# Two attention mixers: head units taken one at a time, or in pairs of partition halves

## The reference, cut to what matters

```
def attend(q, k, v):                      # even mixer: 8 heads on 2 key heads, all 512 keys
    s = einsum('bqhgd,bkhd->bhgqk', q, k) # context queries: 256 context keys alone
    return einsum('bhgqk,bkhd->bqhgd', softmax(s), v)

def block(b, qblk):                       # window mixer: 16 heads on 4 key heads
    s_win = where(valid, q @ k_window, -1e30)     # 128 before, 128 own, 128 after
    s_ctx = q @ k_context                         # 256 keys
    p = softmax(concat([s_win, s_ctx, sink_column]))[..., :-1]
    return p_win @ v_window + p_ctx @ v_context
```

## Time and profile before

| what | us |
|---|---|
| median of 3 runs | 2731.23 (2728.13 to 2741.21) |
| profiled execution, its own time | 2731.92 |
| its span | 2730.1 |
| PE busy | 2486.5 (91%), mean granted clock 0.956 |
| DVE busy | 1493.4 (55%) |
| ACT busy | 902.1 (33%) |
| first to last attention product, even mixer | about 949 to 1124 |
| the same, window mixer | about 2353 to 2482 |

### The profile page before, as it was taken

One profiled execution on the slowest core, in us unless ns is written; L12 is line 12 of the kernel. 1 busy time (PEld: TensorE's weight loads), 2 busy tenths in 40 slices (PEclk: granted clock), 3 DMA queues, 4 the chain that ended last, 5 costly groups with the idle time before them and its releaser, 6 DMA issues.

```text
span 2730.1 us, 41787 instructions
## 1 busy us (share of the span) xinstructions
PE 2486.5 (91%) x17450; PEld 2000.5 (73%) x17450; DVE 1493.4 (55%) x2494; ACT 902.1 (33%) x1583; POOL 76.5 (3%) x148
## 2 busy tenths in 40 slices
PE   8999999799998888777987899998999997988998
PEld 6687778588876656577875688876788875656998
DVE  5666474555544666666544655555555443573553
ACT  2331231422322444542223422223322223353542
POOL 0000000000000000000000000000000000000000
PEclk9999999999999999898989999999999998997999
DMA  7236436244444100000012244433444441101553
GB/s 286 93 136 210 169 126 221 102 139 139 140 146 156 60 33 32 0 3 4 4 43 99 104 143 139 139 139 123 139 139 139 142 151 63 62 32 61 179 181 137
DMA packets 55915, 310.78 MB, mean 114 GB/s; under 512 B 5936, under 2 KB 9392, under 8 KB 28080
## 3 DMA queue, kind: packets, MB, share of 16 engines
q1 hardware_dynamic: 32944, 224.74, 23.2%
q0 software_dynamic: 20736, 75.51, 8.4%
q10 hardware_dynamic: 2048, 7.85, 0.8%
HBM read 307.03 MB, written 1.05 MB: 113 GB/s over the span
## 4 chain that ended last, share of the span: by engine, by line
PEld 40%; PE 33%; issue 11%; DVE 9%; ACT 6%; DMA 1%; PEldq 0%; ACTq 0%; DVEq 0%
PEld bank L1293 13%; PEld bank L1286 13%; PEld bank L1289 12%; PE bank L1166 5%; PE bank L1354 3%; PE bank L1163 2%; PE bank L1225 2%; PE bank L1241 2%; PE bank L1030 2%; PE bank L1139 2%; PE bank L1037 2%; PE bank L1033 2%; ACT hn L1712 2%; PE bank L1120 1%; PE bank L1130 1%
## 5 line engine op out<-in xcount | busy, mean ns | idle before, releaser
L2153 DVE TENSOR_TENSOR w_lo<-ring,w_hi 128x1024 fp32r<-128x1024 f32 (+1 forms) x198 | 236.2, 1193 | 447.8 <-ACT w_hi L1677 447.8
L1286 PE MATMUL bank<-ffn_x_hi,w_hi 128*128 128x512 f32 x1008 | 398.7, 396 | 0.0
L1289 PE MATMUL bank<-ffn_x_lo,w_hi 128*128 128x512 f32 x1008 | 398.7, 396 | 0.0
L1293 PE MATMUL bank<-ffn_x_hi,w_lo 128*128 128x512 f32 x1008 | 398.7, 396 | 0.0
L1677 ACT ACTIVATE w_hi<-ring 128x1024 fp32r<-128x1024 f32 (+1 forms) x198 | 203.9, 1030 | 288.5 <-PE bank L1289 277.2
L2085 DVE SCALAR_TENSOR_TENSOR ms<-mod_rows,c_silu 128x1024 f32<-128x1024 f32 x200 | 244.0, 1220 | 1.2
L1293 PEld LDWEIGHTS bank<-ffn_x_hi,w_lo 128*128 128x128 f32 x1008 | 189.5, 188 | 45.7
L1286 PEld LDWEIGHTS bank<-ffn_x_hi,w_hi 128*128 128x128 f32 x1008 | 189.5, 188 | 45.7
L1289 PEld LDWEIGHTS bank<-ffn_x_lo,w_hi 128*128 128x128 f32 x1008 | 189.5, 188 | 45.6
L1286 PE MATMUL bank<-ffn_h_hi,w_hi 128*128 128x512 f32 x528 | 211.3, 400 | 0.0
L1289 PE MATMUL bank<-ffn_h_lo,w_hi 128*128 128x512 f32 x528 | 208.8, 396 | 0.0
(11 more groups left out here) (440 smaller groups left out, 4621.5 us busy)
## 6 DMA issues: line engine op xcount, KB each, us to landing
ring<-in_stream SPq DMA_DIRECT2D x211, 1024.0 KB, 4.8
mod_rows<-in_mod_stream POOLq DMA_DIRECT2D x144, 512.0 KB, 3.8
one_const<-in_one ACTq DMA_DIRECT2D x1, 1665.0 KB, 13.8
mix_const<-in_two ACTq DMA_DIRECT2D x1, 1440.0 KB, 6.2
win_const<-in_win ACTq DMA_DIRECT2D x1, 1089.0 KB, 4.8
x<-in_x SPq DMA_DIRECT2D x4, 256.0 KB, 4.4
c_silu<-in_c SPq DMA_DIRECT2D x1, 1024.0 KB, 9.9
x<-in_x SPq DMA_DIRECT2D x1, 1024.0 KB, 25.7
```

Source lines behind the costliest of these rows:

```text
L1286: mm = pe.matmul(bank[:, 0:tok], w_high, hi, start=k == 0, stop=False)
L1289: mm = pe.matmul(bank[:, 0:tok], w_high, lo, start=False, stop=False)
L1293: mm = pe.matmul(bank[:, 0:tok], w_low, hi, start=False, stop=last)
L2153: V.tensor_tensor(low[:, 0:h.nk, :], raw_half(h), high[:, 0:h.nk, :].bitcast(F32), ALU.subtract).then_inc(sem("w_split"), 1)
```

## The change

Units are reordered so that two that follow each other differ in nothing but the partition half, and `attention` is replaced in both mixers by `attention_pairs`, which takes two of them in one step. The first block keeps `attention`.

- **PE**: scores are cut in column pieces (2 of 256 in the even mixer, 2 of 192 in the window mixer) and issued alternately for the two units, each in its own bank. Value products alternate likewise, into one bank, partitions 0 to 63 and 64 to 127. Order in a step: scores of pair i, values of pair i-lag-1, transposes of pair i-lag (6 or 8 in two banks). Lag is 1 in the even mixer and 2 in the window mixer.
- **Sink and padding** become 2 score columns, a product of 4 rows (`sink_q`, `sink_k`), 2 columns wide: the mask, the maximum and the exponential's sum take them along. The steps on L2310, L2320, L1762 and L1763 go.
- **DVE**: the maximum comes out negated, so the multiplication by -1 (L2311) goes; one reciprocal serves a pair. With lag 1 a step rescales pair i-1 and then takes the maxima of pair i; with lag 2 the other way round.
- **ACT**: one copy takes a pair's product out (128 partitions). `nop`s and waits behind copies and exponentials go.
- **Places**: one pair in each of the places 6 to 17 of the even mixer, finishing steps in 18 and 19; two pairs in each of the places 5 to 10 of the window mixer, 7 steps in the tail.
- The constants of the window mixer grow from 2178 to 2432 columns of 128 partitions.

```diff
+PAIR_LAG = (1, 2)
-        units = [6 + u // 2 for u in range(24)] + [18, 19, 20]
+        pairs = [6 + n for n in range(12)] + [18, 19]
...
-        units = [5 + u // 4 for u in range(24)] + [len(main)] * 11
+        pairs = [5 + n // 2 for n in range(12)] + [len(main)] * 7
...
-            sc = [(ph4["q"][rows, j, cols], ph4["q"][rows, 8 + j // 4, P:TOK], TOK - P, [])]
+            sc = [(ph4["q"][rows, j, cols], ph4["q"][rows, 8 + j // 4, k0:k0 + 192], 192, []) for k0 in (P, P + 192)]
+            sc.append((c4("sink_q")[0:4, cols], param("sink_k", 2 * head, 2)[0:4, :], 2, []))
...
+            def attention_pairs(us, lag):          # PE
+                def step(i):
+                    if i < n:
+                        two = us[2 * i:2 * i + 2]
+                        taken = [take_bank() for _ in two]
+                        at = 0
+                        for k, (_, _, width, _) in enumerate(two[0].scores):
+                            for u, (bank, full) in zip(two, taken):
+                                lhs, rhs, _, _ = u.scores[k]
+                                mm = pe.matmul(bank[:, at:at + width], lhs, rhs, start=True, stop=True)
...
+                    if i >= lag + 1:
+                        j = i - lag - 1
+                        bank, full = take_bank()
+                        for b, use in copied[j]:
+                            pe.wait_ge(bank_free[b], use + 1)
+                        for k in range(len(two[0].outs)):
+                            for a in range(last + 1):
+                                for e, u in enumerate(two):
+                                    mm = pe.matmul(bank[p0:p0 + dv, k * P:(k + 1) * P], v, u.bufs["pT"][:, e, kt * P:(kt + 1) * P],
...
+                    if lag <= i < n + lag:
+                        j = i - lag
+                        pe.wait_ge(sem("pair_ready"), b_p + j + 1)
+                        for e in range(2):
+                            bank, full = take_bank()
+                            for kt in range(u.keys // P):
+                                mm = pe.transpose(bank[:, kt * P:(kt + 1) * P], ...
...
+                def step(i):                        # DVE
+                    if lag == 1 and 1 <= i < n + 1:
+                        rescaled(i - 1)
+                    if i < n:
+                        largest(i)
+                    if lag == 2 and 1 <= i < n + 1:
+                        rescaled(i - 1)
...
+                        V.tensor_reduce(stats[:, (2 * i + e) % 4, 0:u.parts], src, AX_X, ALU.max, negate=True).then_inc(sem("pair_max"), 1)
...
-                        if u.sink is not None:      # ACT
-                            nc.scalar.activation(stats[:, i % 4, 3:4], u.sink, ACT.Exp, bias=stats[:, i % 4, 0:1])
-                            last = nc.scalar.activation(stats[:, i % 4, 6:7], u.pad, ACT.Exp, bias=stats[:, i % 4, 0:1])
```

More of the change, by code:

```diff
@@ L122, in const_tables @@
     padding = np.where(q[:, 1, 0] >= 128, q[:, 1, 0] - 127, 0)
[L123 removed]
+    out["sink_q"] = np.zeros((P, SEQ))
+    out["sink_q"][0], out["sink_q"][1] = 1.0, np.concatenate([np.full(P, MASKED), np.log(padding)])
     out["window"] = np.concatenate([win, np.zeros_like(win)], 2).reshape(P, -1)
@@ L309, in blend_order @@
                     yield what, i
-        for i, place in enumerate(units):
+        for i, place in enumerate(pairs):
             if place == at:
-                yield "unit", i
+                yield "pair", i
         if layer == 0 and at == 19:
@@ L1013, in blend @@
                 steps = blend_steps(layer)
-                norms, scores = head_norms(steps), attention(units)
+                norms, scores = head_norms(steps), attention_pairs(units, PAIR_LAG[layer])
                 b_r = tally("heads_roped", sum(st.rope is not None for st in steps))
@@ L1072, in blend @@
                         norms(what, i)
-                    elif what == "unit":
-                        if i < len(units):
-                            pe.wait_ge(sem("heads_roped"), b_r + blend_needs(layer, i))
-                        if i == 3:
+                    elif what == "pair":
+                        if 2 * i < len(units):
+                            pe.wait_ge(sem("heads_roped"), b_r + blend_needs(layer, 2 * i))
+                        if i == PAIR_LAG[layer] + 1:
                             b, use = held["v"]
@@ L2249, in blend @@
                             turns.next()
-                    elif what == "unit":
-                        scores(i, before != "unit")
+                    elif what == "pair":
+                        scores(i)
                     elif what != "none":
                         norms(what, i)
-                    before = what
             def gated_add(bank, free, layer, v, c, tok):
@@ L2343, in attention, with attention_pairs, largest, rescaled @@
                 return step, came_out
+            def attention_pairs(us, lag):
+                n = len(us) // 2
+                read, slots = {}, 2 * lag + 2
+                def largest(i):
+                    read[i] = []
+                    for e in range(2):
+                        u = us[2 * i + e]
+                        bank, _ = full_bank()
+                        read[i].append(((turns.n - 1) % BANKS, (turns.n - 1) // BANKS))
+                        src = bank[:, 0:u.width].rearrange("p (k w) -> p k w", k=u.parts)
+                        if u.mask is not None:
+                            part = src[:, :, u.mask_at:u.mask_at + u.mask.shape[2]]
+                            link(V.tensor_tensor(part, part, u.mask, ALU.add))
+                        V.tensor_reduce(stats[:, (2 * i + e) % 4, 0:u.parts], src, AX_X, ALU.max, negate=True).then_inc(sem("pair_max"), 1)
+                def rescaled(i):
+                    u, at = us[2 * i], 2 * i % 4
+                    for b, use in read[i]:
+                        dve.wait_ge(bank_free[b], use + 1)
+                    link(V.reciprocal(stats[:, at:at + 2, 4:4 + u.parts], stats[:, at:at + 2, 2:2 + u.parts]))
+                    w = u.keys // u.parts
+                    for e in range(2):
+                        for k in range(u.parts):
+                            pk = u.bufs["p"][:, (2 * i + e) % slots, k * w:(k + 1) * w]
+                            last = V.tensor_scalar(pk, pk, stats[:, at + e, 4 + k:5 + k], None, ALU.mult)
+                    last.then_inc(sem("pair_ready"), 1)
+                def step(i):
+                    if lag == 1 and 1 <= i < n + 1:
[4 more added lines that the diff above has]
+                        rescaled(i - 1)
+                    if i >= lag + 1:
+                        turns.next()
+                    if lag <= i < n + lag:
+                        for e in range(2):
+                            turns.next()
+                return step
             def mixer(layer):
```

113 lines of the change are left out of this document (76 added, 37 removed).

## The result

The changed kernel takes 2666.56 us (median of 4 runs, 2663.92 to 2669.14) against 2732.07 for the kernel before (2728.13 to 2741.21): ratio 0.976, 95% interval 0.974 to 0.978. The gain is 65.5 us; the forecast was 40, and the time lies outside the range. The profiled execution's span is 2666.8 (before 2730.1).

What follows compares the result with a forecast made beforehand. PE, busy 91% of the span, was taken as the bound, with DVE's chain setting mixer places. Window mixer -20.7, -9.1 and -10.8, even mixer 0, constants +0.5 summed to -40: 2692 us, range 2680 to 2700.

Steps and rivals of the forecast that it cites:

- the same 0.23 each as anywhere in the feed-forward stages: Dense halves of the window mixer: 5.57 us over 24 products, read as full rate, against a clock staying at 1.2 GHz.
- place 5: Window mixer: the lag of two leaves fewer products before the dense half; 9.7 us saved, less 0.6 carried over: -9.1.
- places 6 to 10: Window mixer: DVE's path (6.29 us) ends after PE's (6.03); 4.1 saved in each of five places, -20.7.
- tail: End of the window mixer: from 32.8 us to 22, between 18.6 at full clock and 26.8; -10.8.
- Value products: Attention pairs on PE: the two column halves run side by side, 0.80 us a pair instead of 1.46.
- Even mixer: DVE's chain sets its places: -1.5 us from the pairs, +1.5 for the clock after longer waits, 0 together.
- Load of constants: Head of the window mixer: 12% more columns hold DVE up by 0 to 0.9 us; +0.5 taken.
- Serial values: Rival, window mixer: value products of a pair run one behind another; +10 us, 2702; chance 0.17.
- no overlap: Rival, window mixer: neither scores nor values of a pair overlap on PE; +20 us, 2712; chance 0.05.
- the clock that stays down: Rival: PE stays at 1.2 GHz through the window mixer; +66 us, 2758; chance 0.03.
- The clock takes back: Rival: tail slow as before in share (+4.8 us), clock falls in the even mixer (+3.9); 2701; chance 0.13.

Runs made afterwards that it cites:

- before_64: The kernel before with 16 unused columns (64 bytes) ending the parameter tile, so later tensors lie as in the changed kernel: 2701.65 us, ratio 0.988.
- ffn_64: The kernel before with 64 unused bytes ahead of the feed-forward tensors alone, weights unmoved: 2703.04 us, ratio 0.989.
- micro: No computation: TensorE alone runs 72 products of 512 columns at each of 18 positions of moving operand and weights; 226.9 ns each at distance 0, 233.3 at -64.
- all_64: The kernel before with 64 unused bytes ahead of the split weights, so weights and feed-forward tensors move together: 2737.23 us, ratio 1.001.
- no_alt: The changed kernel, but PE issues all scores of one unit, then of the other, and values likewise, without alternation: 2688.09 us, ratio 0.983.
- even_single: The changed kernel with the even mixer's attention units one by one and the old lag, window mixer still in pairs: 2661.72 us, ratio 0.974.
- micro2: No computation: TensorE alone, 21 cases of operand distance, split format and full 32-bit products of several widths; 32-bit products of 512 columns take 429.2 ns at each distance.
- old_sink: The changed kernel with the window mixer's sink and padding back on VectorE and ScalarE, as in the kernel before: 2686.82 us, ratio 0.984.

## Why the prediction was wrong

**The step that failed** is the sum itself: "-20.7 - 9.1 - 10.8 + 0 + 0.5 = -40" has no term for what the change does to addresses. I had read the wider tile of parameters as columns to load and no more. It moves the feed-forward inputs from 192 to 0 bytes past a multiple of 256, counted from their weights (77,760 and 77,824 bytes, estimated from the order and the sizes of the tensors), and that is worth 32 us (before_64; 28 in ffn_64, where those tensors alone move). With the 33 to 35 of the rest of the change this makes the 65.5. The prediction had the clue in hand and rounded it away: a dense half is "the same 0.23 each as anywhere in the feed-forward stages". It was 0.227 in the mixers and 0.233 in the feed-forward stages, 6 ns on 4608 instructions. The Trainium skill (TensorE: Matmul & The Clock Gate, Part 2: What happens when you issue a matmul) says that TensorE has two independent read ports, so that "Loading the next tile's weights doesn't steal SBUF read bandwidth from the running matmul." The micro rows do not bear that out: with TensorE alone at work, the distance between the two operands changes the rate by 6.4 ns in 227.

**The rest of the sum** was near, and in part by luck. At equal addresses the medians give 35.1 (before_64 to the changed kernel) where the sum says 40. The window mixer was to give 40.6. It gave 45.0 against the kernel before and 40.4 against before_64, but the parts don't come out one by one:

| part of the window mixer | forecast | against before | against before_64 |
|---|---|---|---|
| place 5 (now 9.28) | -9.1 | -9.6 | -9.4 |
| places 6 to 10 (four of 12.14 to 12.34, one of 6.85) | -20.7 | -22.5 | -25.6 |
| tail (now 20.0) | -10.8, bounds -14.2 and -6.0 | -12.8 | -5.4 |

The changed kernel's mixer took 115.4 or 115.5 in all five traces that have it. The old one took 160.4 (before), 155.8 (before_64), 153.1 (ffn_64) and 165.7 (all_64), one execution of each, with the same instructions. Its tail takes 32.8 or 32.9 at a granted clock of 0.69 in before and in all_64, and 25.4 at full clock in ffn_64 and in before_64, whose tail is this (columns as above):

```profile
2422.53:2447.88 25.35, 21.58 (x115) 12.65 (x114) 19.90 (x67) 17.61 (x59) 0.00 (x0) 1.00 0.00 1
```

In return place 6 of before_64, partly at the lower level (0.83), takes 19.9 instead of 16.8. Where the clock falls shifts for causes that this study doesn't name, so the gain is 38 to 50 by the trace that it is held against, and that one of them gives the forecast to 0.2 is luck. In the steady places the sum had DVE later (6.29 to PE's 6.03); it came out the other way by a little, 6.13 for PE without a wait and about 6.04 for DVE with the same 0.14 to reach PE. With the dense half 0.63 behind the start of the transposes instead of 0.80, a place is 12.3 instead of 12.7. The tail's work at full clock was put at 18.6 and took 20.0; the clock never fell there, and I had given it half of the loss.

**Value products** of both column halves ran side by side, 0.81 a pair. The Trainium skill's rule (TensorE: Matmul & The Clock Gate, Part 3), by which a weight load that shares its rows does not overlap, would have made it 1.46 by the prediction's estimate; the trace disagrees. Even in no_alt they took 1.08.

**Even mixer**: 0 forecast, 0 at equal addresses (233.0 to 232.9), and the wait of 4.51 for 4.4. Against the kernel before it is +3.0. The old code takes 233.0 in before_64 too (most of the difference is in place 13), 233.2 in all_64 and 231.3 in ffn_64, one execution each; even_single, with the same units one by one, takes 233.0. So the longer times are those where the mixer's tensors lie 64 bytes further, but whether addresses or scatter of the clock make these 3 us is open. The working saw that the chain through DVE sets the places, but did not ask what the second lag, which it had just priced at 9 us in place 5 of the window mixer, would do here: 48.5.

**Load of constants**: DVE's idle time for it went from 7.54 to 7.99, +0.45 for +0.5.

**Rivals.** Serial values, no overlap and the clock that stays down are refuted by rows above. (The last was priced with dense halves at twice their time, where the other terms use 1.83 times; that would be 61 instead of 66.) "The clock takes back" did not come in the tail, which has full clock. In the even mixer it came: over places 11 to 14 the granted clock is 0.81, against 0.92 in the kernel before and 0.87 in before_64.

## What to carry to other kernels

When a diff changes the width of any tile, list what is allocated behind it, and compare the start-to-start time of the largest matmul groups at full nanoseconds, never rounded: a cost that no dependency shows can stand in every one of thousands of instructions. For work that is put between dense halves, count the steps between its scores and its transposes before its instructions: one more pair of lag was worth 19.8 us of the window mixer and 48.5 of the even one. Where two engines finish a place within 0.3 us of each other, moving small work from one to the other is no free trade.

## What the hardware showed

- TensorE's rate for products of 512 columns in the split parts' format (float32r) depends on the distance between moving operand and weights in a partition: 227 ns at 0, 229 at 64, 232.5 at 128, 233.3 at 192, 236 at -16, and again 227 at 256, -256, 512 and 1024 bytes (micro, micro2). With 256 columns it is 119.9 at 0 and 113.8 at 192. Full 32-bit products take the same at 0, 64, 128 and 192 (429.2 with 512 columns, 215.8 with 256).
- Instructions of four rows and two columns cost 0.13 us each (0.53 for a pair's four) between products of other shapes, and here replace work that costs more on VectorE (old_sink, 22.7 us).
- Behind the waits of 4.2 to 4.5 us in places 11 to 14 of the even mixer, the transposes take 1.62 instead of 0.85 and the dense half 6.2 to 7.6 instead of 5.6; its products start 0.43 us apart for a time instead of 0.23 (1034.58 to 1037.99 in the trace). Behind waits of 1.3 to 1.6 in the same mixer both run at full rate (0.85, and 5.6 to 5.7). A wait isn't the only thing that goes before the lower level: in place 5 of no_alt PE had not waited.
